# Split products for the convolution input, the memory norm on ScalarE, and the convolution mean ahead of the turned probabilities

## What is computed

```python
h = rmsnorm(x, norm_mix_g)
proj = h @ w_in                       # q, k, v (512 each), forget (8), conv a and gate (512 each)
attn = forgetting_attention(q, k, v, log_sigmoid(forget + b))   # causal, 8 heads of 64
z = (a + b_a) * sigmoid(gate + b_g)   # then causal depthwise convolution, 31 taps, 512 channels
conv = silu(layernorm(z_conv) * g + b)
x = x + concat([rmsnorm(attn), conv]) @ w_out
mem_n = rmsnorm(mem, mem_norm_g)
k, v = split(mem_n @ w_mkv)           # keys and values of the memory attention
...                                   # queries, softmax, w_mo; 32 experts, top 2; the second block
```

## Time and profile before

| | us |
|---|---|
| median of 3 runs | 1246.65 (1245.35 to 1247.71) |
| span of the profiled execution | 1243.5 |
| what the median has above that span | 3.15 |
| PE busy, share of the span | 1087.6, 87% |
| DVE busy | 625.0, 50% |
| ACT busy | 448.7, 36% |
| start of the output projection (L756) | 146.66 |

### The profile page before, as it was taken

The page is one execution under the profiler, slowest core; times in us unless marked ns, Lnnn a source line. Parts: engine busy times, 40 slices in busy tenths (PEclk is TensorE's granted clock), DMA queues, the critical chain, the costliest instruction groups (busy, mean ns, idle before and its releaser), DMA issues.

```text
span 1243.5 us, 17193 instructions
## 1 busy us (share of the span) xinstructions
PE 1087.6 (87%) x7361; PEld 784.0 (63%) x7361; DVE 625.0 (50%) x1022; ACT 448.7 (36%) x691; POOL 9.2 (1%) x19
## 2 busy tenths in 40 slices
PE   9999999898575667665758999999999999999998
PEld 7987898743121132121314987878886688888886
DVE  5998845620000000000003698896478666775476
ACT  5246534210000000000004656656587634554353
POOL 0000000000000000000000100000000000000000
PEclk9999999999878788787879999999999999999999
DMA  9543395599999999999999454555544064455430
GB/s 371 204 154 137 152 372 211 227 418 434 425 435 427 432 430 428 435 428 432 429 424 413 169 169 140 168 170 169 193 162 188 21 242 172 175 197 203 169 135 35
DMA packets 23582, 332.45 MB, mean 267 GB/s; under 512 B 2752, under 2 KB 3152, under 8 KB 5072
## 3 DMA queue, kind: packets, MB, share of 16 engines
q1 hardware_dynamic: 22448, 328.14, 66.0%
q0 software_dynamic: 1056, 3.18, 0.8%
HBM read 330.26 MB, written 1.05 MB: 266 GB/s over the span
## 4 chain that ended last, share of the span: by engine, by line
PE 65%; DMA 17%; DVE 7%; ACT 5%; another core or an unknown queue 3%; issue 2%; DVEq 0%; SPq 0%; ACTq 0%
DMA homes<-in_w_up 11%; PE ps L693 10%; PE ps L756 9%; PE ps L1461 7%; PE ps L656 6%; DMA homes<-in_w_down 6%; PE ps L1085 6%; PE ps L675 4%; PE ps L1113 4%; PE ps L896 2%; PE ps L677 2%; PE ps L785 2%; ACT arena L2451 2%; PE ps L1060 2%
## 5 line engine op out<-in xcount | busy, mean ns | idle before, releaser
L1085 PE MATMUL ps<-homes,arena 128*32 128x512 f32 x1024 | 157.0, 773 | 87.2 <-DMA homes<-in_w_up 48.2
L1602 DVE TENSOR_TENSOR parts<-ring,parts 128x2048 fp32r<-128x2048 f32 x70 | 160.0, 2291 | 73.1 <-ACT parts L2484 72.4
L2484 ACT CAST parts<-ring 128x2048 fp32r<-128x2048 f32 x70 | 133.2, 1905 | 141.2 <-PE ps L656 54.2
L693 PE MATMUL ps<-parts 128*128 128x512 f32 x768 | 181.0, 393 | 2.9 <-DVE parts L1602 2.8
L1942 DVE TENSOR_TENSOR arena<-arena,ps 128x512 f32<-128x512 f32 x8 | 5.5, 687 | 338.8 <-PE ps L1085 338.8
L1085 PEld LDWEIGHTS ps<-homes,arena 128*32 128x32 f32 x1024 | 38.9, 137 | 203.1 <-issue 108.9
L693 PEld LDWEIGHTS ps<-parts 128*128 128x128 f32 x768 | 142.3, 188 | 35.2 <-issue 5.6
L756 PE MATMUL ps<-parts 128*128 128x512 f32 (+1 forms) x600 | 136.2, 384 | 0.9 <-DVE parts L1609 0.6
L756 PEld LDWEIGHTS ps<-parts 128*128 128x128 f32 x600 | 108.2, 188 | 25.4 <-issue 3.7
L1113 PE MATMUL ps<-homes,arena 128*32 128x512 f32 x512 | 66.6, 665 | 24.8 <-DMA homes<-in_w_down 22.2
L1461 PE MATMUL ps<-parts 128*128 128x512 f32 x384 | 87.3, 389 | 0.0
(11 more groups left out here) (392 smaller groups left out, 1355.8 us busy)
## 6 DMA issues: line engine op xcount, KB each, us to landing
ring<-in_units SPq DMA_DIRECT2D x35, 2048.0 KB, 8.3
homes<-in_w_up SPq DMA_DIRECT2D x13, 4096.0 KB, 44.7
homes<-in_w_gate SPq DMA_DIRECT2D x11, 4096.0 KB, 43.3
ring<-in_units SPq DMA_DIRECT2D x37, 1024.0 KB, 5.3
homes<-in_w_down SPq DMA_DIRECT2D x9, 4096.0 KB, 44.8
homes<-in_w_down SPq DMA_DIRECT2D x7, 2048.0 KB, 16.0
homes<-in_w_gate SPq DMA_DIRECT2D x5, 2048.0 KB, 12.1
spare<-in_units SPq DMA_DIRECT2D x5, 2048.0 KB, 8.0
```

The source lines that it names most:

```text
L693: mm = nc.tensor.matmul(banks[t], v[:, 4 * h + k, t * P:t * P + P], w[:, k, :], start=h + k + n == 0, stop=h == 1 and k == 3 and n == 2)
L1085: mm = nc.tensor.matmul(ps[e * CAP:e * CAP + CAP, bank, :], picked[:, 2 * u + k, e * CAP:e * CAP + CAP], w(e, k), start=u + k == 0, stop=u ...
L1602: step(V.tensor_tensor(rest_half(name, h), split_half(name, h), w_high[stage][h].bitcast(F32), ALU.subtract), f"{stage}_rest_ready", wait= ...
L2484: step(S.copy(w_high[stage][h], split_half(name, h)), f"{stage}_high_ready", wait=False)
```

## The change

Three of the four column groups of the convolution input are made as split products. ScalarE casts them and VectorE subtracts (one instruction of 128x2048 each). The memory's norm, sums of squares and scalings, goes to ScalarE. Five kinds of evictions (q, the odd quarters of the turned memory, memory keys 0 and 1) go from VectorE to ScalarE. The convolution's mean and squares stand ahead of the turned probabilities on VectorE and TensorE. The variance's factor, epsilon and root become one ScalarE instruction. The transposes of the attention output stand after 4 steps of memory values 1 (they stood after 8). Several semaphores that counted one thing each are merged into one that counts on.

```diff
+        split_columns = [("conv_a", 0), ("conv_g", 1), ("conv_a", 1)]
+        column_high = [grid(parts_of_page[n][:, :], KT) for n in (24, 25, 15)]
...
+        def column_rest(name, c):
+            return grid(parts_of_page[2 * unit_at[name][1] + c][:, :], KT)
...
-                        if n == 7 and between:
+                        if n == 3 and between:
...
                 for c in range(2):
                     for name in BY_COLUMNS:
...
+                        if (name, c) in split_columns:
+                            at = split_columns.index((name, c))
+                            pe.wait_ge(sem("x_rest_ready"), 1)
+                            pe.wait_ge(sem("column_rest_ready"), at + 1)
+                            terms = [(column_high[at], mix_high), (column_rest(name, c), mix_high), (column_high[at], mix_rest)]
...
-                for blk in blocks1:
-                    turn_probs(blk)
                 pe.wait_ge(sem("consts_landed"), 16)
...
                 channel_sums("conv_mean", conv)
+                for blk in blocks1:
+                    turn_probs(blk)
...
-                dve.wait_ge(sem("mem_landed"), 16)
-                normalize(mem_tok, mem_normed, 0, "mem_normed")
+                for n, (name, c) in enumerate(split_columns):
+                    dve.wait_ge(sem("column_high_ready"), n + 1)
+                    step(V.tensor_tensor(column_rest(name, c), grid(column_half(name, c), KT), column_high[n].bitcast(F32), ALU.subtract),
+                         "column_rest_ready", wait=False)
+                dve.wait_ge(sem("mem_squared"), TT)
+                mem_factor = stat(2, 2)
+                step(V.tensor_scalar(mem_factor, stat(0, 2), 1.0 / D, EPS, ALU.mult, ALU.add), "variance_ready", wait=False)
+                roots.append(mem_factor)
+                dve.wait_ge(sem("root_ready"), len(roots))
+                step(V.reciprocal(mem_factor, mem_factor), "mem_factor_ready", wait=False)
...
                 convolve(range(8, 11), range(2, 4))
-                for f in range(2):
-                    bank = filled_by(dve, f"q{f}")
-                    drain(V.tensor_copy(qT1[:, 2 * f:2 * f + 2, :], grid(bank, 2)), f"q{f}")
                 split_rest("mixer", 1, 1)
                 convolve(range(11, 13))
                 split_rest("mixer", 2, 0)
                 convolve(range(13, 15))
-                turned("memT", memT, "mem_norm_g")
                 split_rest("mixer", 2, 1)
...
-                split_rest("mixer", 5, 0)
+                bank = filled_by(dve, "conv_mean")
+                mean = decay[:, 0:T]
                 for blk in blocks1:
                     inverse_sums(blk)
+                drain(V.tensor_scalar(mean, bank[:, 0:T], 1.0 / D_CONV, None, ALU.mult), "conv_mean", wait=True)
+                step(V.tensor_tensor(conv, conv, wide(mean.unsqueeze(1), [P, 4, T]), ALU.subtract))
+                step(V.tensor_tensor(glu, conv, conv, ALU.mult), "conv_ready", wait=False)
+                for blk in blocks1:
                     probs_turned(blk)
-                split_rest("mixer", 5, 1)
+                for h in range(2):
+                    split_rest("mixer", 5, h)
...
-                drain(V.tensor_scalar(mean, bank[:, 0:T], 1.0 / D_CONV, None, ALU.mult), "conv_var", wait=True)
-                step(V.tensor_scalar(mean, mean, EPS, None, ALU.add), "variance_ready", wait=False)
-                inverse_root(mean)
+                drained_by(dve, "conv_var")
+                step(V.reciprocal(mean, mean))
...
+                for n, (name, c) in enumerate(split_columns):
+                    act.wait_ge(sem(f"half_landed{2 * unit_at[name][1] + c}"), 16)
+                    step(S.copy(column_high[n], grid(column_half(name, c), KT)), "column_high_ready", wait=False)
                 channel_gates(0)
+                act.wait_ge(sem("mem_landed"), 16)
+                for t in range(TT):
+                    step(S.activation(mem_normed[:, t, :], mem_tok[:, t, :], ACT.Square, accum_out=stat(t, 1)), "mem_squared", wait=t == TT - 1)
                 root()
-                for h in range(2):
-                    split_high("mixer", 0, h)
+                split_high("mixer", 0, 0)
+                act.wait_ge(sem("mem_factor_ready"), 1)
+                split_high("mixer", 0, 1)
+                for t in range(TT):
+                    step(S.activation(mem_normed[:, t, :], mem_tok[:, t, :], ACT.Copy, scale=stat(2 + t, 1)), "mem_normed", wait=False)
...
-                root(3)
+                root(2)
+                bank = filled_by(act, "conv_var")
+                drain(S.activation(decay[:, 0:T], bank[:, 0:T], ACT.Sqrt, scale=1.0 / D_CONV, bias=stat(508, 1)), "conv_var")
```

More of the change, by code:

```diff
@@ L895, in _ @@
                             for k in range(KT):
[L896 to L897 removed]
+                                for n, (w, v) in enumerate(terms):
+                                    mm = nc.tensor.matmul(bank[:, half * T:half * T + T], w[:, k, half * P:half * P + P], v[:, k, :],
+                                                          start=k + n == 0, stop=k == KT - 1 and n == len(terms) - 1)
                         close_bank(mm, f"{name}{c}")
                         unit_last_fill[name] = f"{name}{c}"
[L900 removed]
+                pe.wait_ge(sem("x_rest_ready"), 1)
                 split_feature_major("q", "q", mix_high, mix_rest)
@@ L1564, in half_turned @@
                     drain(ins, f"{tag}{t}1")
[L1566 to L1574, removed]
                 def softmax(blk):
@@ L1631, in inverse_sums @@
                     step(V.reciprocal(inv, sums))
+                step(V.memset(stat(508, 1), EPS), wait=False)
                 step(V.memset(page(8, 0, T // 2 + 1), 0.0), "first_bits_ready", wait=False)
@@ L1723, in _ @@
                 convolve(range(18, 22))
[L1725 to L1732, removed]
+                convolve(range(22, 27))
                 split_rest("mixer", 4, 0)
                 convolve(range(27, 29))
-                for f in range(2):
-                    memory_keys(1, f)
                 split_rest("mixer", 4, 1)
@@ L2430, in turned @@
                 def turned(tag, dst, gain=None):
-                    for j in (0, 2):
+                    for j in range(4):
                         bank = filled_by(act, f"{tag}{j}")
@@ L2512, in _ @@
                 drained_by(act, *[f"mixT{t}{f}" for t in range(TT) for f in range(2)])
-                step(S.copy(mix_high, xT), "mixer_x_high_ready", wait=False)
+                step(S.copy(mix_high, xT), "x_high_ready", wait=False)
                 def channel_gates(f):
@@ L2527, in _ @@
                     split_high("mixer", 1, h)
+                for f in range(2):
+                    bank = filled_by(act, f"q{f}")
+                    drain(S.copy(qT1[:, 2 * f:2 * f + 2, :], grid(bank, 2)), f"q{f}")
                 for f in range(2):
@@ L2535, in _ @@
                 drained_by(act, *[f"memT{j}" for j in range(4)])
-                step(S.copy(mem_high, memT), "mem_x_high_ready", wait=False)
+                step(S.copy(mem_high, memT), "x_high_ready", wait=False)
                 tmp = page(4, 0, 1024)[0:HEADS, :].rearrange("p (n t) -> p n t", n=4)
@@ L2543, in _, with memory_keys @@
                     copy_out(f"v{t}", v1[:, t, :])
+                def memory_keys(c):
+                    for f in range(2):
+                        bank = filled_by(act, f"mem_k{c}{f}")
+                        drain(S.copy(mem_k[:, 4 * c + 2 * f:4 * c + 2 * f + 2, :], grid(bank, 2)), f"mem_k{c}{f}")
+                act.wait_ge(sem("key_bias_ready"), 2)
+                memory_keys(0)
                 for h in range(2):
                     split_high("mixer", 4, h)
+                memory_keys(1)
                 for h in range(2):
@@ L2577, in _ @@
                 drained_by(act, *[f"normT{t}{f}" for t in range(TT) for f in range(2)])
-                step(S.copy(cross_high, xT), "cross_x_high_ready", wait=False)
+                step(S.copy(cross_high, xT), "x_high_ready", wait=False)
                 top2, sum2 = grid(stat(16, 8), TT), grid(stat(24, 8), TT)
```

45 lines of the change are left out of this document (16 added, 29 removed).

## The result

Measured side by side, the kernel before took 1246.12 us (median of 15 runs, 1244.33 to 1248.30) and the changed one 1251.43 us (15 runs, 1246.81 to 1253.16). The ratio is 1.0034, 95% interval 1.0024 to 1.0043. The forecast was no change, 1246.8 us, range 1244.6 to 1249.0: wrong.

What follows compares the result with a forecast made beforehand. TensorE bounds to about 115 us, then VectorE and ScalarE with TensorE close behind, up to the output projection's start. -3.6 (columns) + 2.3 (k's rest) + 1.4 (forget sums) = +0.1 us: 1246.8 us, range 1244.6 to 1249.0.

Steps and rivals of the forecast that it cites:

- Step 1: Convolution input: three split column groups save 3 x 1.21 = 3.6 us, so q starts at 35.1.
- The square: ScalarE's Square of 128x1024 in the memory's norm, in no profile row, taken as 1.05 us.
- rival C: ScalarE late with the memory's norm if table loads cost 1.4 us more than the rows show: 1248.8 us, chance 0.08.
- The landing: Convolution input's last columns land about 11.4 us after their issue at 3.5 to 4.0, by some 16.5 us.
- Steps 2 and 3: TensorE waits 2.3 us for k's first rest, then 1.6 us before the forget product, at 66.3 against 66.15.
- Step 4: Keys 0 and 1 to scores: moving keys' evictions to ScalarE gives TensorE no wait, cost 0.
- Step 5: Mean ahead of the probabilities: VectorE's 1.27 us saving is covered by TensorE; output projection starts 0.1 us later than before.
- The term around the span: The 3.15 us between the profiled span and the median of the runs, added to the span of 1243.6.
- Rival D: TensorE's clock falls at new idle spells before k and the forget product: 1249.3, up to 1250.2 us, chance 0.09.

Runs made afterwards that it cites:

- the gap filled: Changed kernel with 12 small unread products in TensorE's idle 1.54 us ahead of the products of probabilities and values: 1247.91 us, 1.0014 of before.
- the order undone: Changed kernel with turned probabilities ahead of the mean again on TensorE and VectorE: 1251.54 us, 1.0044 of before.
- the longer gap: Changed kernel with one rest of memory values 1 ahead of the turned probabilities on VectorE: 1255.59 us, 1.0074 of before.
- the order alone: Kernel before with only the mean ahead of the turned probabilities, both rests of memory values 1 behind them: 1250.17 us, 1.0027 of before.
- the gap left open: Changed kernel with k's rests earlier and forget sums evicted first, gap ahead of the 64-column products not filled: 1244.34 us, 0.9985 of before.

## Why the prediction was wrong, point by point

Step 1 (columns, -3.6) was right: q starts at 35.15, and plain columns cost 3.6 us again. The square took 1.05 us, as chosen. The slower table loads of rival C did not come: 23.41 + 1.28 = 24.69, next instruction at 24.70. The landing "by some 16.5" does not follow from its own terms (4.0 + 11.4 = 15.4); ScalarE's third cast had to wait for its columns until 16.98. It did no harm: the last rest still ended at 21.65, wanted at 29.4.

Steps 2 and 3 were right: 2.40 for 2.3 us, 1.50 for 1.6. The forget product was 0.66 us late where I had 0.1: q landed 0.14 later, TensorE started k 0.14 after its rest was done, and k took 0.25 longer than half of the 23.03 us of both. With k's rests and the forget sums moved, the forget product came 3.4 us earlier than before the change and the output projection 3.6.

Step 4 was right, no wait.

**Step 5 is where it failed.** Its sequence was right (mean's sum, gap, products, values 1, TensorE last), but all its durations were those of 2.4 GHz, and a fall of the clock at this place was put at nothing, in the sum and among the rivals. The gap was in the sum without a line of its own: by its terms the mean's sum and the transposes end at 125.6, and the products "start at about 127.1". Measured, it is 1.54 us, ahead of the 64-column products; before the change 1.20 us stood ahead of the transposes. Behind the new gap the clock fell: from 127.84 to 138.99 TensorE needed 11.2 us for what took 134.14 - 126.84 = 7.3 before, 3.9 us; the first 12 products of values 1 add 0.75 (3.87 for 3.12 us at full clock). With the 0.7 by which 127.84 was later than 127.1, less about 0.5 because TensorE no longer had to wait for the second attention output, that is the start at 151.8 for 146.8.

**The term around the span** was mis-sized as well, 3.15 us for 1.8. It hid in the median of three runs, and made the lower group look like the forecast.

**Rival D** had the right mechanism, the wrong place (49 and 66), a price of 1.7 to 3.5 us from falls of 3.5 to 7 us, where this fall lasted 10.2, and a chance of 0.09. In its own place the fall came too, in three profiles of four, and at 130, by the times, in ten executions of fifteen. The argument against it, that 2.3 us idle is shorter than what came before 247, was the error: one case that fell at a longer idle time says nothing on what a shorter one does. Four profiles have the same front (the changed kernel, the gap filled, the order undone, the longer gap: all edits lie behind it). At 47 the clock fell behind gaps of 2.08, 1.97 and 2.17 us, and not behind the longest, 2.40 us in the changed kernel; behind the gap of 1.5 us at 65 it fell in none of the four. The length of the gap alone does not decide.

The start of the second block moved from 679.4 to 685.9 between the two profiles, 5.1 us of it by the output projection. The other 1.4 arose behind it and is not explained. Single executions differ there in both directions: with the order alone the output projection started 4.5 us late and the span was only 2.9 us longer, with the order undone 3.8 and 2.3. Where the fall at 130 was avoided, the medians followed the start of the output projection to about 1 us.

What stays open: why some executions fall and others don't at the same gap; whether the gap of 1.20 us before the change is harmless by its length or by its place ahead of transposes; and whether the one-group result of the order alone is a matter of its position or of seven runs.

## What to carry to other kernels

Follow a reordering on TensorE not only by which wait ends last but by where its idle time goes: here about 1.5 us of it in front of the 64-column products cost four to five more, though 1.2 us in front of the transposes had cost none. When the times of a kernel fall into two groups, look in a profile of the upper one for a granted clock under 1.00, and fill the gap ahead of it with small products that nobody reads: if the upper group goes, that was it. A time that lands on the forecast is no proof of the sum; the starts and spans of the trace are. A faster producer only pays when the hand-written order behind it is moved too: here 3.6 us were there, and lay in k's rests, which stood three taps too late, and in one eviction that stood behind eight others.

## What the runs showed that I had not expected

A gap of 1.5 us was enough for 10.2 us at 1.2 GHz, and not in every execution: by the groups of times, 10 of 15 in the changed kernel, 6 of 12 in the one with the gap left open, none with the gap filled. The Trainium skill (TensorE: Matmul & The Clock Gate, HAM oscillation) has idle gaps throttle the clock, and the gaps it describes are longer than this one. The trace agrees on the mechanism: the clock went from 1.00 to 0.50 behind 1.54 us idle. By the times, that came in part of the executions only. Twelve products of 128x256 in bf16 took 1.47 us and the clock stayed at 1.00 behind them in all six profiles that have them, at no cost in time, since TensorE had been idle there anyway.
